# Stick-breaking sums with the later key blocks added up on VectorE first, and the scores copied out of PSUM by ScalarE

## The chip, the cores and the metric

The kernel runs on one core of a Trainium2 chip. Its time is the device time of one execution in microseconds (us), and lower is better. Three runs of the kernel before gave 1179.3, 1180.42 and 1184.48 us, a median of 1180.42. One further execution was recorded by the profiler and took 1179.15 us.

The core has five engines with a queue each, which they work off in order: TensorE (PE in the rows; its weight loads are PEld), VectorE (DVE), ScalarE (ACT), GpSimd (POOL) and SyncE (SP, which issues DMAs). They wait for one another through semaphores. `x.wait_ge(s, n)` holds engine x until semaphore s has reached n, and `.then_inc(s, 1)` raises it when the instruction is done.

## The reference, cut to what matters

The program is one inference step of a hybrid encoder layer: a large input projection, stick-breaking attention (8 heads), a state-space branch, a merge, cross-attention to memory tokens, and a mixture of 16 experts. The change lies in stick-breaking attention alone:

```python
z = jnp.einsum('bqhd,bkhd->bhqk', qb, k_all).astype(f32) * scale
causal = k_pos[None, :] < q_pos[:, None]
log_keep = jnp.where(causal, jax.nn.log_sigmoid(-z), 0.0)
after = lax.cumsum(log_keep, axis=3, reverse=True) - log_keep
w = jnp.where(causal, jnp.exp(jax.nn.log_sigmoid(z) + after), 0.0)
return jnp.einsum('bhqk,bkhd->bqhd', w.astype(v_all.dtype), v_all)
```

For each query, `after` is the sum of log_keep over all later keys up to the query. With l = softplus(z) = -log_keep, the weight is w = exp(z - S), where S at a key is the sum of l over that key and all later ones. There are 512 prompt tokens, and 64 sample tokens that also see 512 cached keys.

## The kernel before, in words

Keys lie on the 128 partitions and queries along the row. A **unit** u is one piece of this work, 1280 values wide. Units 0 to 7 are the eight heads of the prompt: four key blocks kc of 128 keys, for which only the queries from block kc on count, so they are 512, 384, 256 and 128 wide. Units 8 and 9 are the sample tokens, four heads each, with five key blocks of 256 columns. `keycols(u, kc)` gives the place and width of a block. A unit passes through these steps:

- `scores(u)`, TensorE, lines 2875 to 2896: z into PSUM, columns 0 to 1279.
- `z_copy(u)`, VectorE, line 2190: z out of PSUM into `ZSB[u % 6]`.
- `mask(u)`, GpSimd, lines 1664 and 1668: entries that aren't causal get a large negative number.
- `softplus_log(u)`, ScalarE, lines 1819, 1821 and 1823: Abs, Exp and Ln into `LB[u % 2]`.
- `log_sum(u)`, VectorE, line 2194: max(z, 0) is added, which makes l.
- The copy of l, rounded to the format of the fast product (fp32r), into `LBH[u % 2]`, GpSimd, line 1677. `log_low(u)`, VectorE, line 2200, then leaves the rest, l minus its rounded copy, in `LB`. A product with both is nearly as exact as fp32.
- `sums(u)`, TensorE, lines 2911, 2915 and 2916: S into PSUM, columns 1536 to 2815. For key block kc this is a product of a triangle of ones with the block's own l, and a product of a full matrix of ones with each later block j. A block of 256 or more columns takes two fp32r products (high, low); the last one, 128 wide, is a plain fp32 product. That is 12 fp32r and 4 fp32 products in units 0 to 7, and 30 fp32r products in units 8 and 9.
- `u_op(u)`, VectorE, line 2207: z - S. Exp of it by ScalarE, line 1829. `values(u)`, TensorE, line 2928: the product with V for two units.

All engines walk the units in one loop over i, with fixed offsets. TensorE at step i does scores(i), sums(i - 2), then filling work (rows of V by `v_rows`, line 2765, while i < 5), and at even i from 4 on values(i - 4). scores(i) waits until z_copy(i - 1) has emptied its PSUM columns. VectorE does log_low(i - 2), z_copy(i), log_sum(i - 1), u_op(i - 2). ScalarE does the Exp of unit i - 3, softplus_log(i), then the copies of filling work (`kv_out`, line 1786) and at i = 2 and 6 a rounding of a weight tile (line 486, `split_high`). GpSimd does mask(i), then the rounded copy of unit i - 1. At i = 4 the last v_rows has to be copied out by ScalarE before values(0) starts. At i = 10 and later TensorE does `x_rows`, products of the next stage (line 2765 too); x_rows(3) is the first one behind the loop.

## Time and profile before

| what | before |
|---|---|
| runs | 1179.3, 1180.42, 1184.48 us |
| profiled execution, its own time | 1179.15 us |
| its span, first instruction to last | 1177.4 us |
| TensorE busy | 1122.1 us, 95% |
| VectorE busy | 805.8 us, 68% |
| ScalarE busy | 608.2 us, 52% |
| GpSimd busy | 124.5 us, 11% |
| attention loop | from 79.9 us (scores(0)) to 209.15 us (x_rows(3)) |

A row of the timeline has the start in us, the length in us, engine, line, operation, output and inputs, and how many instructions are merged in it. In brackets stands how long the engine had been idle, and who ended that. A TensorE instruction is shown with its latency, so neighbours overlap: what one costs is the distance to the next start. The granted clock 1.00 is 2.4 GHz; lower means are stretches partly at 1.2 GHz.

### The profile page before, as it was taken

Reading aid. Unit: us, or ns where it says so; the run is one execution under the profiler, and the core shown is the slowest. Engines: PE = TensorE matmul, PEld = TensorE weight load, DVE = VectorE, ACT = ScalarE, POOL = GpSimd, SP = SyncE. Lnnn points to the kernel's source line nnn. Section 1 sums busy time; section 2 is a strip of 40 time slices with the busy share of each in tenths; the row PEclk is TensorE's granted clock in tenths of the full one; section 3 lists DMA queues with packets and bytes.
Section 4 is the critical chain, followed back from the end, with each engine's and each line's share of the span. In section 5 each row is a group of like instructions: output and inputs, shape, how many; then the busy total and the mean of one; then the engine's idle time right before and its main releaser. Section 6 shows DMA issues by size and latency. Waiting matters only on the chain.

```text
span 1177.4 us, 18680 instructions
## 1 busy us (share of the span) xinstructions
PE 1122.1 (95%) x7757; PEld 1014.3 (86%) x7766; DVE 805.8 (68%) x993; ACT 608.2 (52%) x807; POOL 124.5 (11%) x148
## 2 busy tenths in 40 slices
PE   6999999999999899899999999999899999999995
PEld 6988789999987799899999999989767878788884
DVE  6324665865968887987535733534589998899895
ACT  6334463335397576643215523312166768677773
POOL 2002431000245000000000000000001000000032
PEclk9999999999999999999999999999799999999998
DMA  9431110323120344442627602201799999999988
GB/s 300 136 120 37 37 41 1 109 72 121 30 55 1 87 123 117 133 151 76 220 72 239 225 3 72 73 1 55 292 353 382 421 419 386 375 400 390 375 274 200
DMA packets 94655, 205.26 MB, mean 174 GB/s; under 512 B 4336, under 2 KB 70040, under 8 KB 81640
## 3 DMA queue, kind: packets, MB, share of 16 engines
q1 hardware_dynamic: 85792, 173.88, 41.6%
q0 software_dynamic: 5584, 19.81, 5.7%
q10 hardware_dynamic: 3192, 10.34, 2.2%
q8 instruction: 63, 1.03, 0.4%
q14 instruction: 24, 0.20, 0.0%
HBM read 182.41 MB, written 21.61 MB: 173 GB/s over the span
## 4 chain that ended last, share of the span: by engine, by line
PE 75%; DVE 9%; ACT 8%; issue 4%; DMA 3%; ACTq 0%; POOL 0%; SPq 0%; DVEq 0%; POOLq 0%
PE ps L2765 34%; PE ps L3101 10%; PE ps L1112 6%; DVE buf_r L1046 4%; ACT buf_r L1039 3%; PE ps L1122 3%; PE ps L3290 2%; PE ps L3306 2%; DMA buf<-in_w_gate_e 1%; PE ps L2886 1%; ACT buf_r L507 1%; DVE buf_r L1261 1%; PE ps L2915 1%; PE ps L2928 1%; PE ps L2916 1%
## 5 line engine op out<-in xcount | busy, mean ns | idle before, releaser
L2765 PE MATMUL ps<-buf_r,buf_r 128*128 128x288 f32 (+1 forms) x3312 | 435.7, 291 | 6.2 <-ACT buf L1812 2.6
L2765 PEld LDWEIGHTS ps<-buf_r,buf_r 128*128 128x128 f32 x3312 | 423.4, 189 | 10.3 <-issue 6.7
L1046 DVE TENSOR_TENSOR buf_r<-buf,buf_r 128x2048 fp32r<-128x2048 f32 x92 | 205.1, 2284 | 0.0
L1112 PE MATMUL ps<-buf_r,buf_r 128*128 128x512 f32 x720 | 174.6, 397 | 0.0
L1039 ACT CAST buf_r<-buf 128x2048 fp32r<-128x2048 f32 x92 | 170.8, 1909 | 0.0
L1112 PEld LDWEIGHTS ps<-buf_r,buf_r 128*128 128x128 f32 x720 | 133.2, 188 | 29.7 <-issue 0.5
L3101 PE MATMUL ps<-buf_r,buf_r 128*128 128x288 f32 x1008 | 140.2, 299 | 9.3 <-ACT buf L1977 4.4
L3101 PEld LDWEIGHTS ps<-buf_r,buf_r 128*128 128x128 f32 x1008 | 137.3, 192 | 11.1 <-issue 9.2
L492 DVE TENSOR_TENSOR buf_r<-buf,buf_r 128x2048 fp32r<-128x2048 f32 (+1 forms) x33 | 74.5, 2262 | 36.2 <-ACT buf_r L486 36.1
L486 ACT CAST buf_r<-buf 128x2048 fp32r<-128x2048 f32 (+1 forms) x37 | 69.7, 1883 | 56.7 <-PE ps L2789 39.7
L1122 PE MATMUL ps<-buf_r,buf_r 128*128 128x512 f32 x384 | 89.8, 389 | 0.5 <-DVE buf_r L1289 0.5
L1122 PEld LDWEIGHTS ps<-buf_r,buf_r 128*128 128x128 f32 x384 | 72.0, 188 | 15.8 <-DVE buf_r L1289 0.9
L507 ACT CAST buf_r<-ps 128x512 fp32r<-128x512 f32 (+2 forms) x41 | 30.0, 731 | 75.8 <-PE ps L1096 63.2
L2365 DVE TENSOR_TENSOR buf_r<-buf,buf_r 128x512 fp32r<-128x512 f32 (+1 forms) x60 | 53.1, 911 | 7.8 <-ACT buf_r L1895 3.3
L638 ACT ACTIVATE buf<-buf 128x1024 f32<-128x1024 f32 (+1 forms) x22 | 23.2, 1056 | 36.7 <-DVE buf L2686 18.7
L1312 POOL DMA_INDIRECT buf<-hn_rows,buf x16 | 17.2, 1073 | 233.9 <-DVE buf L706 133.6
L2190 DVE COPY buf<-ps 128x1280 f32<-128x1280 f32 x10 | 14.9, 1491 | 36.9 <-PE ps L2886 31.8
L507 ACT CAST buf_r<-buf 128x1024 fp32r<-128x1024 f32 (+4 forms) x20 | 19.0, 948 | 40.8 <-DVE buf L2515 34.1
L1702 POOL TENSOR_TENSOR buf<-buf,buf 128x1024 f32<-128x1024 f32 x10 | 28.6, 2863 | 53.0 <-ACT buf L1930 53.0
L1819 ACT ACTIVATE buf<-buf 128x1280 f32<-128x1280 f32 x10 | 12.7, 1274 | 40.1 <-POOL buf L1664 31.0
L1261 DVE TENSOR_TENSOR buf_r<-ps,buf_r 128x1024 fp32r<-128x1024 f32 x15 | 18.4, 1225 | 18.7 <-ACT buf_r L507 18.7
L2104 ACT ACTIVATE buf<-ps 128x288 f32<-128x288 f32 x16 | 6.6, 410 | 46.8 <-PE ps L2765 46.8
(367 smaller groups left out, 1521.6 us busy)
## 6 DMA issues: line engine op xcount, KB each, us to landing
buf<-in_w_gate_e SPq DMA_DIRECT2D x32, 1024.0 KB, 8.2
buf<-in_w_up_e SPq DMA_DIRECT2D x32, 1024.0 KB, 7.5
buf<-in_w_down_e SPq DMA_DIRECT2D x32, 1024.0 KB, 7.6
buf<-in_w_in SPq DMA_DIRECT2D x16, 1024.0 KB, 5.5
buf<-in_w_in SPq DMA_DIRECT2D x17, 512.0 KB
buf<-in_w_mem_kv SPq DMA_DIRECT2D x8, 1024.0 KB, 6.2
y_rows<-buf ACTq DMA_DIRECT2D x14, 512.0 KB, 7.1
buf<-in_x_prompt SPq DMA_DIRECT2D x8, 512.0 KB, 5.3
```

The lines of the kernel that those rows point to most:

```text
L486: nc.scalar.copy(w_hi(n), tile_view(RAW[n % NRAW], n)).then_inc(wh_ready, 1)
L492: nc.vector.tensor_tensor(r32(raw), raw, w_hi(n), ALU.subtract).then_inc(wl_ready, 1)
L507: nc.scalar.copy(r32(hi), src).then_inc(ah_ready, 1)
L1039: nc.scalar.copy(e_hi(t), e_raw(t)).then_inc(wh_ready, 1)
L1046: nc.vector.tensor_tensor(e_lo(t), e_raw(t), e_hi(t), ALU.subtract).then_inc(wl_ready, 1)
L1112: last = nc.tensor.matmul(bank(b), r32(a[:, k, :]), w[:, i, :], start=(k == 0 and j == 0), stop=(k == KD - 1 and j == 2))
L1122: last = nc.tensor.matmul(bank(5 + c), r32(a[:, k, :]), w[:, i, 512 * c:512 * (c + 1)], start=(k == 0 and j == 0), stop=(k == 3 and j == 2))
L1261: nc.vector.tensor_tensor(r32(GT[e % 2]), bank(0, 2).rearrange("p (c n) -> p c n", c=KD), r32(GTH[e % 2]), ALU.subtract).then_inc(al_ready, 1)
L1702: nc.gpsimd.tensor_tensor(CE[v % 2], CE[v % 2], bc(XC[:, 10 + g, c * P:(c + 1) * P].unsqueeze(1), [P, 8, P]), ALU.mult).then_inc(ce_ready, 1)
L2365: return nc.vector.tensor_tensor(r32(out), raw, r32(high), ALU.subtract).then_inc(m_low, 1)
L2765: last = nc.tensor.matmul(out, a, b, start=(k == 0 and j == 0), stop=(k == len(parts) - 1 and j == 2))
L3101: last = nc.tensor.matmul(out, r32(a[:, k, :]), r32(b[:, k, :]), start=(first and k == 0 and j == 0), stop=(k == 3 and j == 2), skip_group ...
```

## The change

After `log_sum`, VectorE adds the key blocks that lie later, column block by column block, into 512 more columns of `LB`. `sums(u)` then takes one product with ones per key block on these added-up columns, in place of one per later block. The rounded copy and `log_low` work on the longer tile. GpSimd now waits for four signals per unit (`RAW_STEPS`). The copy of z out of PSUM moves from VectorE's queue to ScalarE's, ahead of the Exp of unit i - 3. The tiles `LB`, `LBH` and one of `ZSB` lie elsewhere in memory, which brings waits on `mt_stored`, the end of a store of an earlier stage (issued at 53.75 us in the trace).

```diff
-        LB = [A.view(1280) for _ in range(2)]
+        LATER = 512
+        LB, LBH = [A.view(1280 + LATER)], [A.view(1280 + LATER)]
+        A.back(base)
+        LB.insert(0, A.view(1280 + LATER))
+        LBH.insert(0, A.view(1280 + LATER))
         ZSB.append(A.view(1280))
-        A.back(base)
-        LBH = [A.view(1280) for _ in range(2)]
...
+        def sums_later(u, kc):
+            if u < SBH:
+                return {0: [(1408, 3, P)], 1: [(1024, 2, 2 * P)], 2: [(896, 1, P)], 3: []}[kc]
+            return {0: [(256, 2, P), (1536, 2, P)], 1: [(1536, 2, P)], 2: [(1280, 2, P)], 3: [(1024, 2, P)], 4: []}[kc]
...
+                    pool.wait_ge(mt_stored, 16)
+                    pool.wait_ge(sp_raw, RAW_STEPS * u + RAW_STEPS)
+                    nc.gpsimd.tensor_copy(r32(LBH[u % 2]), LB[u % 2]).then_inc(lh_ready, 1)
...
+            def z_copy(u):
+                act.wait_ge(z_psum, u + 1)
+                if u == 3:
+                    act.wait_ge(mt_stored, 16)
+                if u == 4:
+                    act.wait_ge(out_stored, 16 * 2)
+                if u >= 6:
+                    act.wait_ge(pv_psum, 2 * ((u - 6) // 2 + 1))
+                nc.scalar.copy(ZSB[u % 6], ps[:, 0:1280]).then_inc(z_copied, 1)
...
             for i in range(U_ + 3):
+                if i < U_:
+                    z_copy(i)
                 if i >= 3:
...
             def log_sum(u):
                 dve.wait_ge(l_ready, u + 1)
+                lb, done = LB[u % 2], RAW_STEPS * u
+                nc.vector.scalar_tensor_tensor(out=lb[:, 0:1280], in0=ZSB[u % 6], scalar=0.0, in1=lb[:, 0:1280],
                                                op0=ALU.max, op1=ALU.add).then_inc(sp_raw, 1)
+                dve.wait_ge(sp_raw, done + 1)
+                if u < SBH:
+                    nc.vector.tensor_copy(lb[:, 1408:1536], lb[:, 512:640]).then_inc(sp_raw, 1)
+                    nc.vector.tensor_tensor(lb[:, 1280:1408], lb[:, 1152:1280], lb[:, 896:1024], ALU.add).then_inc(sp_raw, 1)
+                    dve.wait_ge(sp_raw, done + 3)
+                    pair_ = lambda at, step: lb[:, at:at + 2 * step].rearrange("p (b n) -> p b n", n=step)[:, :, 0:P]
+                    nc.vector.tensor_tensor(pair_(1536, P), pair_(640, P), pair_(1024, 2 * P), ALU.add).then_inc(sp_raw, 1)
+                else:
+                    nc.vector.tensor_tensor(lb[:, 1280:1536], lb[:, 768:1024], lb[:, 1024:1280], ALU.add).then_inc(sp_raw, 1)
+                    dve.wait_ge(sp_raw, done + 2)
+                    nc.vector.tensor_tensor(lb[:, 1536:1792], lb[:, 512:768], lb[:, 1280:1536], ALU.add).then_inc(sp_raw, 2)
...
-                for k0, k1 in ((0, 896), (1024, 1280)) if u < SBH else ((0, 1280), ):
+                for k0, k1 in ((0, 896), (1024, 1792)) if u < SBH else ((0, 1792), ):
...
             for i in range(U_ + 2):
                 if i >= 2:
                     log_low(i - 2)
-                if i < U_:
-                    z_copy(i)
                 if 1 <= i <= U_:
                     log_sum(i - 1)
...
-                    for j in range(kc, nk):
...
+                    nc.tensor.matmul(own, TSUF_R, high[:, o:o + n], start=True, stop=False)
+                    last = nc.tensor.matmul(own, TSUF_R, low[:, o:o + n], start=False, stop=(kc == nk - 1))
+                    parts = sums_later(u, kc)
```

TensorE, sums(0), all its products. `buf_104_r` is the triangle and `buf_105_r` the ones in fp32r, `buf_58` and `buf_55` are ones and triangle in fp32. Before:

```order
L2915 MATMUL ps<-buf_120_r,buf_104_r 128x512
L2916 MATMUL ps<-buf_117_r,buf_104_r 128x512
L2915 MATMUL ps<-buf_120_r,buf_105_r 128x384
L2916 MATMUL ps<-buf_117_r,buf_105_r 128x384
L2915 MATMUL ps<-buf_120_r,buf_105_r 128x256
L2916 MATMUL ps<-buf_117_r,buf_105_r 128x256
L2911 MATMUL ps<-buf_117,buf_58 128x128
L2915 MATMUL ps<-buf_120_r,buf_104_r 128x384
L2916 MATMUL ps<-buf_117_r,buf_104_r 128x384
L2915 MATMUL ps<-buf_120_r,buf_105_r 128x256
L2916 MATMUL ps<-buf_117_r,buf_105_r 128x256
L2911 MATMUL ps<-buf_117,buf_58 128x128
```

This is key blocks 0 and 1; two fp32r products and two fp32 ones follow for blocks 2 and 3. After, again from the start of sums(0), with all of its products:

```order
L2937 MATMUL ps<-buf_120_r,buf_104_r 128x512
L2938 MATMUL ps<-buf_119_r,buf_104_r 128x512
L2947 MATMUL ps<-buf_120_r,buf_105_r 128x384
L2947 MATMUL ps<-buf_119_r,buf_105_r 128x384
L2937 MATMUL ps<-buf_120_r,buf_104_r 128x384
L2938 MATMUL ps<-buf_119_r,buf_104_r 128x384
L2950 MATMUL ps<-buf_120_r,buf_105_r 128x256
L2950 MATMUL ps<-buf_119_r,buf_105_r 128x256
L2937 MATMUL ps<-buf_120_r,buf_104_r 128x256
L2938 MATMUL ps<-buf_119_r,buf_104_r 128x256
L2943 MATMUL ps<-buf_119,buf_58 128x128
L2935 MATMUL ps<-buf_119,buf_55 128x128
```

The later blocks of block 0 come in one pair 384 wide, and those of block 1 in one pair 256 wide. Twelve products are left of sixteen: two fp32 ones and a pair 256 wide are gone.

ScalarE, steps 5 and 6 of the loop. Before (1829 is the Exp of unit i - 3, 486 the rounding of a weight tile):

```order
L1829 ACTIVATE buf_116<-buf_116 128x1280
L1819 ACTIVATE buf_118<-buf_123 128x1280
L1821 ACTIVATE buf_118<-buf_118 128x1280
L1823 ACTIVATE buf_118<-buf_118 128x1280
L1829 ACTIVATE buf_119<-buf_119 128x1280
L1819 ACTIVATE buf_117<-buf_114 128x1280
L1821 ACTIVATE buf_117<-buf_117 128x1280
L1823 ACTIVATE buf_117<-buf_117 128x1280
L486 CAST buf_73_r<-buf_71 128x2048
```

After (1834 is the copy of z, 1853 the Exp, 488 the rounding):

```order
L1834 COPY buf_123<-ps 128x1280
L1853 ACTIVATE buf_116<-buf_116 128x1280
L1841 ACTIVATE buf_117<-buf_123 128x1280
L1843 ACTIVATE buf_117<-buf_117 128x1280
L1845 ACTIVATE buf_117<-buf_117 128x1280
L1834 COPY buf_114<-ps 128x1280
L1853 ACTIVATE buf_121<-buf_121 128x1280
L1841 ACTIVATE buf_119<-buf_114 128x1280
L1843 ACTIVATE buf_119<-buf_119 128x1280
L1845 ACTIVATE buf_119<-buf_119 128x1280
L488 CAST buf_73_r<-buf_71 128x2048
```

The copy of z for step i now stands behind everything that ScalarE does in step i - 1.

## Rows read from the trace of the kernel before

**Rows 1.** The page, busy time: engine, us, share of the span, instructions.
```profile
PE 1122.1 (95%) x7757; PEld 1014.3 (86%) x7766; DVE 805.8 (68%) x993; ACT 608.2 (52%) x807; POOL 124.5 (11%) x148
```
**Rows 2.** Busy time by stretch: from:to, length, PE, PEld, DVE, ACT, POOL, PEclk, DMA.
```profile
135.00:150.00 15.00, 13.28 (x59) 8.67 (x60) 8.09 (x8) 5.87 (x7) 3.51 (x6) 0.85 0.19 64
```
**Rows 3.** The chain of waits, loop step 4: start, us, what.
```profile
127.46 1.50 DVE buf L2190
```
**Rows 4.** Timeline of TensorE, sums(0) in step 2.
```profile
105.42 0.50 PE L2915 MATMUL ps<-buf_r,buf_r 128*128 128x512 f32 x1
...
106.58 0.39 PE L2911 MATMUL ps<-buf,buf 128*128 128x128 f32 x2
...
106.98 0.34 PE L2916 MATMUL ps<-buf_r,buf_r 128*128 128x384 f32 x1
...
107.15 0.28 PE L2915 MATMUL ps<-buf_r,buf_r 128*128 128x256 f32 x1
...
107.27 0.28 PE L2916 MATMUL ps<-buf_r,buf_r 128*128 128x256 f32 x1
...
108.21 5.90 PE L2765 MATMUL ps<-buf_r,buf_r 128*128 128x256 f32 x48
```
**Rows 5.** Timeline of TensorE, steps 9 to 13.
```profile
177.75 6.62 PE L2765 MATMUL ps<-buf_r,buf_r 128*128 128x288 f32 x48
187.87 2.38 PE L2928 MATMUL ps<-buf,buf 128*64 128x512 f32 x16
190.18 6.62 PE L2765 MATMUL ps<-buf_r,buf_r 128*128 128x288 f32 x48
200.22 6.52 PE L2765 MATMUL ps<-buf_r,buf_r 128*128 128x288 f32 x48
...
209.15 6.09 PE L2765 MATMUL ps<-buf_r,buf_r 128*128 128x288 f32 x44
```
**Rows 6.** Timeline of all engines, step 4.
```profile
125.00 2.42 PE L2886 MATMUL ps<-buf,buf 64*128 64x512 f32 x8
...
129.10 2.16 POOL L1664 TENSOR_SCALAR_AFFINE_SELECT buf<-buf 128x128 f32<-128x128 f32 x4 [5.56 <-DVE buf L2190]
...
130.14 3.07 PE L2765 MATMUL ps<-buf_r,buf_r 128*128 128x256 f32 x24
...
135.48 3.97 PE L2928 MATMUL ps<-buf,buf 128*64 128x512 f32 x16 [2.26 <-ACT buf L1786]
```
**Rows 7.** The same, steps 5 and 6.
```profile
139.38 2.42 PE L2886 MATMUL ps<-buf,buf 64*128 64x512 f32 x8
...
141.84 1.49 DVE L2190 COPY buf<-ps 128x1280 f32<-128x1280 f32 x1 [7.92 <-PE ps L2886]
...
145.57 1.27 POOL L1677 CAST buf_r<-buf 128x1280 fp32r<-128x1280 f32 x1
...
148.35 0.50 PE L2915 MATMUL ps<-buf_r,buf_r 128*128 128x512 f32 x1 [1.24 <-DVE buf_r L2200]
```
**Rows 8.** Timeline of GpSimd and VectorE, masks of steps 0 and 1.
```profile
83.96 1.03 POOL L1664 TENSOR_SCALAR_AFFINE_SELECT buf<-buf 128x128 f32<-128x128 f32 x4 [29.62 <-DVE buf L2190]
...
96.14 4.21 POOL L1664 TENSOR_SCALAR_AFFINE_SELECT buf<-buf 128x128 f32<-128x128 f32 x4 [11.15 <-DVE buf L2190]
...
97.31 2.38 DVE L492 TENSOR_TENSOR buf_r<-buf,buf_r 128x2048 fp32r<-128x2048 f32 x1
```
**Rows 9.** Groups by line and shape, ScalarE, whole span: count, then busy us and mean ns.
```profile
L1930 ACT ACTIVATE buf<-ps 128x1024 f32<-128x1024 f32 x10 | 10.2, 1022 | 7.5 <-PE ps L3045 7.5
```
**Rows 10.** The same groups, 78 to 212 us, all engines.
```profile
L1819 ACT ACTIVATE buf<-buf 128x1280 f32<-128x1280 f32 x10 | 12.7, 1274 | 40.1 <-POOL buf L1664 31.0 <-POOL buf L1668 6.8 <-PE ps L2911 2.3
...
L2200 DVE TENSOR_TENSOR buf_r<-buf,buf_r 128x896 fp32r<-128x896 f32 x8 | 8.7, 1091 | 3.6 <-POOL buf_r L1677 3.6
...
L1790 ACT COPY buf<-ps 128x512 f32<-128x512 f32 x9 | 4.8, 593 | 13.2 <-PE ps L2861 13.2
...
L2200 DVE TENSOR_TENSOR buf_r<-buf,buf_r 128x256 fp32r<-128x256 f32 x8 | 3.3, 418 | 0.0
```

More of the change, by code:

```diff
@@ L1817, in softplus_log @@
                     act.wait_ge(s_psum, u - 1)
-                lb = LB[u % 2]
+                lb = LB[u % 2][:, 0:1280]
                 nc.scalar.activation(lb, ZSB[u % 6], ACT.Abs).then_inc(z_abs, 1)
@@ L2906, in sums @@
                     o, n = keycols(u, kc)
-                    for j in range(kc, nk):
-                        oj, nj = keycols(u, j)
-                        out = ps[:, 1536 + o + n - nj:1536 + o + n]
-                        if nj == P:
-                            last = nc.tensor.matmul(out, TSUF if j == kc else ONES, LB[u % 2][:, oj:oj + nj],
-                                                    start=(j == kc), stop=(j == nk - 1))
-                        else:
-                            m = TSUF_R if j == kc else ONES_R
-                            nc.tensor.matmul(out, m, high[:, oj:oj + nj], start=(j == kc), stop=False)
-                            last = nc.tensor.matmul(out, m, low[:, oj:oj + nj], start=False, stop=(j == nk - 1))
+                    own = ps[:, 1536 + o:1536 + o + n]
+                    if n == P:
+                        last = nc.tensor.matmul(own, TSUF, LB[u % 2][:, o:o + n], start=True, stop=True)
+                        continue
+                    nc.tensor.matmul(own, TSUF_R, high[:, o:o + n], start=True, stop=False)
+                    last = nc.tensor.matmul(own, TSUF_R, low[:, o:o + n], start=False, stop=(kc == nk - 1))
+                    parts = sums_later(u, kc)
+                    for at, blocks, step in parts:
+                        out = own[:, n - P * blocks:n] if u < SBH else own
+                        if u < SBH and kc == 2:
+                            last = nc.tensor.matmul(out, ONES, LB[u % 2][:, at:at + P], start=False, stop=True)
+                            continue
+                        for a in (high, low):
+                            if step == P:
+                                last = nc.tensor.matmul(out, ONES_R, a[:, at:at + P * blocks], start=False,
+                                                        stop=(a is low and at == parts[-1][0]))
+                            else:
+                                last = nc.tensor.matmul(out.rearrange("p (b n) -> p b n", n=P), ONES_R,
+                                                        a[:, at:at + blocks * step].rearrange("p (b n) -> p b n", n=step)[:, :, 0:P],
+                                                        start=False, stop=(a is low))
                 last.then_inc(s_psum, 1)
```

14 lines of the change are left out of this document (3 added, 11 removed).

## The prediction

> **What bounds the kernel now.** I read the page first: TensorE is busy for 95% of the span [rows 1], so the reader is to see that only time on TensorE, or time for which it waits, can move the end. The second view is the busy time by stretch. The attention loop runs from 79.9 us (scores(0)) to 209.15 us (x_rows(3)), and in its stretch from 135 to 150 us TensorE is busy for 13.28 of 15 us at a mean granted clock of 0.85, so for a part of it at the lower level, 1.2 GHz [rows 2]. The third view is the chain of waits: it stays on TensorE for most of the loop and leaves it at 127.46 us, for the copy of z by VectorE and what follows on it [rows 3]. The fourth is the timeline of the places where it leaves. There are two real stalls. At step 4 values(0) starts at 135.48 after 2.26 us of idleness, released by the last copy of filling work on ScalarE [rows 6]. At step 6 sums(4) starts at 148.35 after 1.24 us, released by log_low(4) on VectorE [rows 7]. From step 7 on TensorE has no idle row at all. So the loop is bound by TensorE's own work, broken by two latency chains of which ScalarE and GpSimd are part. Both sides of the change count: less work for TensorE, and another chain.
>
> **Part 1, fewer products (a gain on TensorE).** In sums(0) the distance from the first fp32 row at 106.58 to the row at 106.98 holds one fp32 product and the start of a 384-wide one. The distance from 106.98 to 107.15 is one 384-wide product, 0.17 us, so the fp32 product costs 0.23 us. From 107.15 to 107.27 is one 256-wide product, 0.12 us. The whole unit takes 105.42 to 108.21, 2.79 us [rows 4]. A unit of 0 to 7 loses two fp32 products and a pair 256 wide: 2 x 0.23 + 2 x 0.12 = 0.70 us; I take 0.68, since the starts are rounded. Eight units: 5.4 us. For the sample units, x_rows(1) starts at 190.18 and takes 6.62, and x_rows(2) starts at 200.22, so the 30 products of sums(9) take 3.42 us, 0.115 each [rows 5]. Ten of thirty go: 1.15 us a unit, 2.3 us for two. Removed in all: 7.7 us of TensorE's work. Nothing is added there. One of the kept pairs reads its columns with a gap between blocks, which no row shows: bounds are 0 and, if such a pair took twice its 0.23 us, 8 x 0.23 = 1.8 us; I take 0, because the number of columns is the same as in the row beside it.
>
> **Part 2, VectorE.** It loses ten copies of 1.49 us [rows 7]. It gains per unit the additions (128, 128 and 256 columns, or twice 256) and 512 more columns in log_low. The 896-wide and the 256-wide rows of log_low differ by 0.67 us for 640 columns, 1.05 ns each [rows 10], so log_low grows by 0.53 us to 1.97. Three additions cost at most 3 x 0.42 = 1.26 us, the whole 256-wide row each, and at least 512 x 1.05 ns = 0.54 us; I take 0.95, the middle, as they wait for each other. VectorE's load stays as it was (-1.49 + 0.53 + 0.95 = 0.0 us a unit). But both sit in the latency from Ln to sums(u).
>
> **Part 3, GpSimd.** The rounded copy goes from 1280 to 1792 columns. By the row, 1.27 us [rows 7], it becomes at most 1.27 x 1.4 = 1.78 and at least 1.27; I take 1.75. Its masks took 2.16 us at 129.10 [rows 6] but 1.03 us at 83.96, where VectorE was idle, and 4.21 us at 96.14, with VectorE's 2.38 us subtraction of two operands beside them [rows 8]. At 129.10 log_sum(3) ran beside them, queued right behind the copy of z. Now the copy of z comes from ScalarE, and log_sum(i - 1) is done earlier, right after Ln of unit i - 1, while ScalarE still copies. So I expect masks nearer 1.03 than 2.16 us except at step 6, where log_sum(5) and its additions fall on them; both ends are kept.
> The Trainium skill ("SBUF — State Buffer", section "SBUF: two separate sides") says that VectorE and GpSimd share a pair of ports as an exclusive lock, held for a whole instruction, and that VectorE operations with two SBUF inputs take part in it. The three mask rows agree with it. The rule speaks against this change, since the added copy and additions are such holders, and by it masks stay at 2.16 us or above wherever they meet; that result is rival B, which is priced from the rows.
>
> **Part 4, ScalarE.** It takes over the copy of z. Its 1024-wide reads of PSUM take 1.02 us [rows 9] and its 512-wide ones 0.59 us [rows 10], so 0.84 ns a column and 1.23 us for 1280. Bounds: 1.02 below, and 1.49 above, VectorE's copy of the same [rows 7]. What is queued behind it: the Exp of unit i - 3, then Abs, Exp and Ln of unit i, 3 x 1.27 = 3.8, with gaps 3.9 us [rows 10]. Who waits for it: mask(i), and scores(i + 1), whose PSUM columns it frees. In its turn it now stands behind all of ScalarE's step i - 1. The new waits on mt_stored cost nothing: the store was issued 26 us before the loop begins (the time stands with the change).
>
> **The walk, with 0.1 us for each hand-over.** Steps 2 to 4 hold three sums; two are done before scores(4), which so starts at 123.6 for 125.00 [rows 6] and ends at 126.0. ScalarE: copy of z(4) to 127.3, Exp of unit 1 to 128.6 (the mask beside it), three functions to 132.4, last kv_out to 132.8. TensorE: sums(2) 2.1, v_rows 2.9, ready at 131.0. Values(0) starts at 132.8, 2.7 us earlier, with 1.8 us of stall for 2.26. I keep the slow clock behind it: its row shows 3.97 us for what takes 2.38 at 187.87 [rows 5, 6].
> Step 5: scores(5) ends at 139.2. Copy of z to 140.5, mask to 141.6, rounded copy to 143.4, log_low(4) to 145.4; sums(4) starts at 145.5, 2.85 us earlier. TensorE was ready at 143.6 (sums(3) 2.1, scores(6) 2.35), so this stall grows from 1.24 to 1.9 us: that chain kept its length, the shorter copy and mask pay for the longer rounded copy and log_low, and TensorE's gain of 0.68 us in sums(3) is lost in it.
> Steps 6 to 9: ScalarE is now nearly as slow as TensorE. Per step it has 1.23 + mask 1.1 to 1.5 + 3.9 + hand-overs, 6.7 us, and 1.9 us more at step 6 (line 486). TensorE stalls about 0.3 us before scores(8) (copy of z(7) done at 156.3), 0.3 before sums(6) and 0.6 before values(4), 1.2 us in all where there was none. From sums(4) to x_rows(0) it was 148.35 to 177.75 = 29.4 us [rows 5, 7]; four sums less, 2.7, and 1.2 more make 27.9. x_rows(0) starts at 173.4, 4.3 us earlier. Sums(8) and sums(9) add 2.3, rounded down to 2.2: x_rows(3) at 202.65 for 209.15.
> **The sum: -6.5 us.** In terms of Part 1: -7.7 for the products, -0.5 for the shorter stall of step 4, +0.7 at step 6, +1.2 for the small stalls, -0.2 of rounding. Behind the loop all work follows TensorE's, so I let the gain pass to the end. The profiled execution's own time is 1179.15, so 1172.6 us. That execution lies 1.3 us under the median of the runs shown (1180.42), within their scatter; I add nothing for it.
>
> **Rivals.**
> A, the forecast: -6.5, own range -8 to -5.
> B, masks held at 2.16 us everywhere by VectorE's additions and log_low. For it: rows 6 and 8. Against it: log_sum comes earlier now. It lengthens each of the chains of steps 4 to 9; the same walk with 2.16 puts x_rows(3) at 206.6, so -2.5 and 1176.6 us.
> C, the small stalls lower the clock again. A fall costs 1.6 us, 3.97 - 2.38 [rows 5, 6]. For it: three new stalls within 8 us. Against it: each is far under the 1.24 us of the smallest one that was followed by slow rows. Two more falls, 3.2 us: -3.3, 1175.8 us.
> D, one of the two falls of before does not come back, since it follows how long TensorE idles: -6.5 - 1.6 = -8.1, 1171 us. The stall of step 4 is shorter than before, which speaks for it; that of step 6 is longer.
> The Trainium skill ("TensorE: Matmul & The Clock Gate", "What's actually happening") says that the gate goes by activity in a window that runs free of the program. By it, where a fall lands is partly chance, and so C and D both stay open though the stalls are nearly the same. The two falls in the trace agree with it as far as two can.
> E, the other side: ScalarE becomes the bound of steps 5 to 9. Its place is the copy of z(i + 1), which waits behind Ln of unit i. Before, it took 35.9 us from the copy of z(5) at 141.84 [rows 7] to x_rows(0) at 177.75 [rows 5], 7.2 a step. The loop is 2.5 us ahead when z(5) is copied and gains 2.2 behind step 9, so it turns slower once these five steps take (35.9 + 4.7) / 5 = 8.1 us each; the walk has 34.1 / 5 = 6.8. With every upper end at once (copy 1.49, mask 2.16, rounded copy 2.3, a fall at each of the five stalls) the walk puts x_rows(3) at 211.4: +2.3, 1181.4 us.
>
> **How the numbers follow.** Chances: A 0.53, D 0.12, B 0.17, C 0.11, E 0.07. The forecast is A's, 1172.6. 0.5% is 5.9 us, about what a measurement of this kernel can tell from no change. All of D and 0.38 of A lie beyond it: 0.50 faster. The rest of A (0.15), B and C make 0.43 for the same, and E 0.07 for slower. The range reaches from 1168.5 (D with both falls gone, -9.7, and a little for the scatter) to 1178.5 (B and C together, -1, about half of E left out).
>
> **What the profile after would show.** Part 1: sums(0) at 2.1 us, start to next start, and sums(9) at 2.3. Part 3: rounded copy 1.75 us; masks near 1.0 (A) or 2.2 (B). Part 4: the copy of z 1.2 us. Walk: values(0) at 132.8, sums(4) at 145.5, x_rows(0) at 173.4, x_rows(3) at 202.7; two stretches below clock 1.00 in the loop (A), one (D), three or more (C). It would be wrong if x_rows(0) came no earlier than 177 (ScalarE's chain longer than I walked it), if the gapped pair were slower than its neighbour, or if x_rows(3) came 6.5 us earlier and the end did not.

## The result and the profile after

| | median | lowest to highest | runs |
|---|---|---|---|
| before | 1181.03 us | 1178.11 to 1184.48 | 8 |
| after | 1174.2 us | 1171.2 to 1176.67 | 8 |

The ratio is 0.9941, with a 95% interval of 0.9924 to 0.9959. By this ratio it takes 7.0 us less than before (5 to 9), the medians are 6.8 us apart, and the forecast was 6.5 us less. The profiled execution took 1174.3 us (before 1179.15), its span is 1172.6 us (before 1177.4). The two profiles are thus only 4.85 us apart. The profile of before lies 1.9 us under the median of its kernel, and this will matter below.

First the page's busy times after, against [rows 1]:

```profile
PE 1116.9 (95%) x7698; PEld 1008.7 (86%) x7698; DVE 805.5 (69%) x1011; ACT 620.6 (53%) x817; POOL 116.7 (10%) x148
```

TensorE lost 5.2 us of busy time, VectorE nothing. ScalarE gained 12.4, ten copies. GpSimd lost 7.8 us although its rounded copies grew by 4.3 (from 12.6 to 16.9): its masks lost 12.

The groups by line and shape, 78 to 206 us, of after (columns as in [rows 10]):

```profile
L1689 POOL CAST buf_r<-buf 128x1792 fp32r<-128x1792 f32 x10 | 16.9, 1689 | 7.0 <-DVE buf L2223 7.0
...
L1834 ACT COPY buf<-ps 128x1280 f32<-128x1280 f32 x10 | 12.3, 1226 | 14.4 <-PE ps L2912 10.5 <-PE ps L2920 3.9
...
L1674 POOL TENSOR_SCALAR_AFFINE_SELECT buf<-buf 128x128 f32<-128x128 f32 x32 | 10.3, 360 | 79.9 <-ACT buf L1834 79.9
```

and the masks of before in the same view:

```profile
L1664 POOL TENSOR_SCALAR_AFFINE_SELECT buf<-buf 128x128 f32<-128x128 f32 x32 | 20.2, 666 | 78.4 <-DVE buf L2190 78.4
```

The 32 masks of the prompt take half the time. The timeline of after, all engines (the loop begins with its first row; L2937 begins a sums unit, L2964 is values, L2791 rows of V or x_rows, L2228 log_low, L2211 log_sum, L2235 u_op, L2240 a copy that VectorE has at step 5 as filling work):

```profile
79.28 2.39 PE L2912 MATMUL ps<-buf,buf 64*128 64x512 f32 x8 [0.92 <-ACT buf L1802]
...
104.83 0.50 PE L2937 MATMUL ps<-buf_r,buf_r 128*128 128x512 f32 x1
...
106.94 5.90 PE L2791 MATMUL ps<-buf_r,buf_r 128*128 128x256 f32 x48
...
131.89 1.49 DVE L2211 SCALAR_TENSOR_TENSOR buf<-buf,buf 128x1280 f32<-128x1280 f32 x1 [0.32 <-ACT buf L1845]
132.16 2.37 PE L2964 MATMUL ps<-buf,buf 128*64 128x512 f32 x16 [1.56 <-ACT buf L1798]
...
136.93 1.23 ACT L1834 COPY buf<-ps 128x1280 f32<-128x1280 f32 x1 [4.81 <-PE ps L2912]
138.30 1.04 POOL L1674 TENSOR_SCALAR_AFFINE_SELECT buf<-buf 128x128 f32<-128x128 f32 x4 [8.73 <-ACT buf L1834]
...
139.20 1.49 DVE L2235 TENSOR_TENSOR buf<-buf,ps 128x1280 f32<-128x1280 f32 x1 [4.90 <-PE ps L2935]
...
139.27 1.70 POOL L1689 CAST buf_r<-buf 128x1792 fp32r<-128x1792 f32 x1
...
140.61 0.68 DVE L2240 COPY buf<-ps 128x512 f32<-128x512 f32 x1
...
141.21 1.95 DVE L2228 TENSOR_TENSOR buf_r<-buf,buf_r 128x896 fp32r<-128x896 f32 x2
...
143.21 0.50 PE L2937 MATMUL ps<-buf_r,buf_r 128*128 128x512 f32 x1 [1.70 <-DVE buf_r L2228]
...
174.53 6.59 PE L2791 MATMUL ps<-buf_r,buf_r 128*128 128x288 f32 x48
...
203.53 6.62 PE L2791 MATMUL ps<-buf_r,buf_r 128*128 128x288 f32 x48
```

The reader is to see five things. Sums(0) takes 104.83 to 106.94, 2.11 us for 2.79 [rows 4]. Log_sum(4) runs at 131.89, five microseconds before the copy of z(5), so the mask at 138.30 has no such VectorE operation beside it and takes 1.04 us for 2.16 [rows 6]. The stalls are 1.56 us at step 4 (2.26 before [rows 6]) and 1.70 at step 6 (1.24 before [rows 7]). And x_rows(3), the first work behind the loop, starts at 203.53 for 209.15 [rows 5]; 0.60 of these 5.62 us come from ahead of the loop, where nothing was changed. Last, what holds sums(4) at step 6: the rounded copy is done at 140.97, but VectorE comes to log_low(4) only at 141.21, straight from u_op(3), which had waited for sums(3), and a copy behind it. So there the chain over mask and rounded copy, which the prediction walked, ended 0.2 us before VectorE's own queue.

Now the clock. Stretches of after (columns as in [rows 2]; in rows of TensorE alone PE, PEclk, DMA share and GB/s are left), then of before:

```profile
135.00:150.00 15.00, 13.30 (x62) 9.50 (x61) 9.31 (x11) 11.30 (x10) 7.06 (x12) 0.89 0.09 33
150.00:165.00 15.00, 15.00 (x82) 12.91 (x82) 10.26 (x14) 12.33 (x10) 4.85 (x7) 0.77 0.16 52
165.00:180.00 15.00, 15.00 (x109) 14.06 (x106) 9.80 (x10) 10.17 (x9) 2.04 (x2) 0.89 0.00 1
...
144.00:145.00 1.00, 1.00 (x5) 0.50 0.00 0
...
159.00:161.00 2.00, 2.00 (x7) 0.50 0.00 0
...
171.00:173.00 2.00, 2.00 (x6) 0.50 0.00 0
```

```profile
150.00:165.00 15.00, 15.00 (x99) 12.49 (x98) 10.28 (x10) 10.98 (x9) 7.81 (x12) 0.92 0.23 80
165.00:180.00 15.00, 15.00 (x115) 13.32 (x115) 10.63 (x9) 8.15 (x8) 5.46 (x4) 1.00 0.00 1
```

A clock of 0.50 is 1.2 GHz. From such rows I add up the time at the lower level: a stretch of mean clock c has a share 2 x (1 - c) of it. Before it is 6.8 us in the loop, behind the two stalls. After it is 13.6: 3.4 from 143.7, 6.8 from 157.2, 3.4 from 171. In the last two TensorE has no idle row. At 1.2 GHz its work takes nearly twice as long: sums(6) of after, all of it at the lower level, took 4.14 us (159.67 to 163.81) for the 2.32 of sums(5) at full clock (151.67 to 153.99), so 0.44 of such time is lost. I count half, the upper end: 6.8 us lost for 3.4 before. The loop times without the low clock are so too short by up to 0.4 us for before, 0.8 for after and 1.0 for a kernel with 17 us. With the clock taken out (length less half of the low stretch) the loop goes from 129.27 - 3.4 = 125.9 to 124.25 - 6.8 = 117.4 us, 8.4 less; the clock gives 3.4 of it back, and 5.0 are left in this pair of profiles. (With 0.44 in place of a half it is 8.0 less and 3.0 back.)

### The profile page after: what moved, and what is told of

The parts are those of the page before. It is cut to its first block, busy times and chain, and to the rows that moved or that the text cites. A ratio compares the mean times of both kernels' runs of the same rounds, so it can differ in the third digit from the quotient of the medians.

```text
span 1172.6 us, 18594 instructions
## 1 busy us (share of the span) xinstructions
PE 1116.9 (95%) x7698; PEld 1008.7 (86%) x7698; DVE 805.5 (69%) x1011; ACT 620.6 (53%) x817; POOL 116.7 (10%) x148
## 3 DMA queue, kind: packets, MB, share of 16 engines
q8 instruction: 63, 1.03, 0.4%
## 4 chain that ended last, share of the span: by engine, by line
PE 74%; DVE 10%; ACT 9%; issue 4%; DMA 3%; ACTq 0%; SPq 0%; POOL 0%; DVEq 0%; POOLq 0%
PE ps L2791 34%; PE ps L3137 10%; PE ps L1122 6%; DVE buf_r L1056 4%; ACT buf_r L1049 4%; PE ps L1132 3%; PE ps L3326 2%; PE ps L3342 2%; PE ps L2912 1%; ACT buf_r L509 1%; DVE buf_r L1271 1%; PE ps L3105 1%; PE ps L1106 1%; PE ps L2920 1%; PE ps L3108 1%
## 5 line engine op out<-in xcount | busy, mean ns | idle before, releaser
L2791 PE MATMUL ps<-buf_r,buf_r 128*128 128x288 f32 (+1 forms) x3312 | 435.7, 291 | 6.2 <-ACT buf L1824 2.6
L2791 PEld LDWEIGHTS ps<-buf_r,buf_r 128*128 128x128 f32 x3312 | 423.4, 189 | 10.3 <-issue 6.7
L2235 DVE TENSOR_TENSOR buf<-buf,ps 128x1280 f32<-128x1280 f32 x10 | 14.9, 1489 | 28.4 <-PE ps L2935 20.4
L2287 DVE SCALAR_TENSOR_TENSOR buf<-buf,buf,buf 128x579 f32<-128x579 f32 x36 | 29.6, 822 | 1.3
```

The lines of the kernel that those rows point to most:

```text
L2287: o = nc.vector.scalar_tensor_tensor(out=cv[:, 0:579], in0=xr[:, j:j + 579], scalar=CW[:, j, i:i + 1], in1=cv[:, 0:579], op0=ALU.mult, op1 ...
L2791: last = nc.tensor.matmul(out, a, b, start=(k == 0 and j == 0), stop=(k == len(parts) - 1 and j == 2))
```

## The experiments

Each kernel had 6 or 12 runs, with 17 to 29 of before beside them; the ratio is to those, whose medians were 1181.1 to 1181.52 us (for after it is to the 8 above). The table has what the profiles show of the loop, from the start of scores(0) to that of x_rows(3). "Stalls" are TensorE's idle times before values(0) and sums(4).

| kernel | loop | low clock | loop without it | stalls | median | ratio to before, 95% |
|---|---|---|---|---|---|---|
| before | 129.27 | 6.8 | 125.9 | 2.26, 1.24 | 1181.03 | |
| after | 124.25 | 13.6 | 117.4 | 1.56, 1.70 | 1174.2 | 0.9941 [0.9924, 0.9959] |
| e0_changed_again | 124.76 | 13.6 | 118.0 | 1.56, 1.70 | 1174.64 | 0.9942 [0.9927, 0.9957] |
| e1_copy_only | 131.41 | 13.6 | 124.6 | 1.46, 1.17 | 1180.1 | 0.9988 [0.9976, 1.0] |
| e2_sums_only | 128.76 | 17.0 | 120.3 | 3.20, 3.23 | 1181.46 | 0.9996 [0.9982, 1.001] |
| e3_old_products | 130.47 | 10.2 | 125.4 | 1.47, 1.70 | 1181.52 | 1.0005 [0.999, 1.0019] |
| e4_fill_stalls | 123.09 | 10.2 | 118.0 | 0.17, none | 1173.27 | 0.9932 [0.9911, 0.9952] |
| e5_late_log_sum | 129.13 | 17.0 | 120.6 | 3.06, 3.10 | 1181.47 | 0.9997 [0.9986, 1.0009] |
| e6_kv_early | 121.38 | 10.2 | 116.3 | none | 1174.03 | 0.9936 [0.9921, 0.9951] |
| e7_fill_scores | 130.63 | 17.0 | 122.1 | 0.17, none | 1181.28 | 1.0001 [0.9988, 1.0014] |
| e8_split_sums | 124.69 | 13.6 | 117.9 | 1.57, 0.83 | 1174.33 | 0.9942 [0.9925, 0.9958] |
| e9_split_kv_early | 121.70 | 10.2 | 116.6 | none, 0.83 | 1172.93 | 0.993 [0.9914, 0.9946] |
| e10_before_filled | 130.80 | 10.2 | 125.7 | 0.40, none | 1180.18 | 0.9989 [0.9972, 1.0006] |

The rest of the program adds scatter of its own: scores(0) starts between 79.06 and 82.52, though nothing ahead of it differs. So verdicts go by the medians, and the loop's columns explain them as far as one profile can. Every run also lists the mean granted clock of its whole execution. The medians are 0.980 for e2, 0.9795 for e5, 0.982 for e7, 0.9825 for after, 0.985 for e0, 0.983 to 0.9855 for the others and 0.984 to 0.986 for before.

### e1_copy_only

Before, with the copy of z on ScalarE, ahead of the Exp of unit i - 3. The added lines are ScalarE's, the removed ones VectorE's.

```diff
+            def z_copy(u):
...
+                nc.scalar.copy(ZSB[u % 6], ps[:, 0:1280]).then_inc(z_copied, 1)
...
-                if i < U_:
-                    z_copy(i)
```

> The kernel before with one thing moved: ScalarE copies z out of PSUM, at the place in its queue that the change gives it. Sums, additions and rounded copies are as before. Theory 'work' (the gain is TensorE's fewer products, so this half alone brings little): x_rows(3) 1 to 2 us earlier than before, ratio to before 0.998 to 1.000. Theory 'chain' (the gain is the shorter way from scores to values: a shorter copy, masks at 1.0 instead of 2.2 us): 5 us or more, ratio 0.996 or less. Masks at 1.0 us under both.

Measured 0.9988, 0.1%. The masks fall as they do in after:

```profile
141.11 1.05 POOL L1664 TENSOR_SCALAR_AFFINE_SELECT buf<-buf 128x128 f32<-128x128 f32 x4 [9.49 <-ACT buf L1820]
```

The stalls shrink by 0.9 us together, and without the low clock the loop is 1.3 us shorter. So this half alone shortens a wait and little else: it is what theory 'work' expected of it. The stall of step 6 shrinks by only 0.07 us (1.24 to 1.17) although mask and copy of z are 1.4 us shorter, so that path didn't hold it there.

### e2_sums_only

After, with the copy of z back on VectorE between log_low(i - 2) and log_sum(i - 1). The removed lines are ScalarE's, the added ones VectorE's.

```diff
-                if i < U_:
-                    z_copy(i)
...
                     log_low(i - 2)
+                if i < U_:
+                    z_copy(i)
                 if 1 <= i <= U_:
                     log_sum(i - 1)
```

> The changed kernel with the copy of z back on VectorE, between log_low(i - 2) and log_sum(i - 1). The additions and the shorter sums stay. Theory 'work': most of the gain stays, 4 to 6 us, ratio 0.995 to 0.997, with longer stalls at steps 4 and 6 since masks go back to 2.2 us. Theory 'chain': under 2 us, ratio 0.998 or more.

Measured 0.9996: the fewer products alone give nothing. Theory 'work' wanted 0.995 to 0.997 and is missed here, though e1 and e3 fit it: neither of the two theories holds alone. Its timeline, all engines:

```profile
121.14 3.32 POOL L1689 CAST buf_r<-buf 128x1792 fp32r<-128x1792 f32 x1 [0.37 <-issue]
...
130.83 1.48 DVE L2243 TENSOR_TENSOR buf<-buf,ps 128x1280 f32<-128x1280 f32 x1
131.04 1.68 POOL L1689 CAST buf_r<-buf 128x1792 fp32r<-128x1792 f32 x1
...
135.28 3.44 PE L2974 MATMUL ps<-buf,buf 128*64 128x512 f32 x16 [3.20 <-ACT buf L1798]
...
141.68 1.49 DVE L2214 COPY buf<-ps 128x1280 f32<-128x1280 f32 x1 [6.97 <-PE ps L2922]
143.09 1.48 DVE L2219 SCALAR_TENSOR_TENSOR buf<-buf,buf 128x1280 f32<-128x1280 f32 x1
143.32 2.42 POOL L1674 TENSOR_SCALAR_AFFINE_SELECT buf<-buf 128x128 f32<-128x128 f32 x4 [10.60 <-DVE buf L2214]
```

VectorE copies z, then starts log_sum at 143.09, and the mask, which waited for the same copy, starts at 143.32 and takes 2.42 us. Both stalls grow to 3.2 us, 3.2 more together than in after. The low clock grows to 17.0 us, 10.2 more than in the profile of before.

### e3_old_products

After, with the old products (one per later block), so that only TensorE's saving is missing.

```diff
-                    parts = sums_later(u, kc)
...
+                    for j in range(kc, nk):
+                        oj, nj = keycols(u, j)
+                        out = ps[:, 1536 + o + n - nj:1536 + o + n]
```

> The changed kernel with additions, longer rounded copy, longer log_low and ScalarE's copy, but TensorE's sums take one product per later block as before (the added-up columns are made and not used). Theory 'work': the gain falls to about 1 us, ratio 0.999 (0.998 to 1.001); the difference to the changed kernel is the price of 7.7 us of products. Theory 'chain': ratio stays at 0.994 to 0.996.

Measured 1.0005: taking the products back costs the whole gain. Without the low clock its loop is 8.0 us longer than that of after and 7.4 longer than that of e0 (the forecast's term: 7.7).

### e0_changed_again

The changed kernel once more, for a second profile of it.

> The changed kernel as it is, a second profile and more runs on the chip of this call. Ratio to before 0.992 to 0.996. Falls of the clock behind scores(8) and scores(9) again, if these cause them; elsewhere, if they come by chance.

Ratio 0.9942, the same. Its low clock in the loop is 13.6 us again, but placed otherwise: 157 to 167 and 174 to 178, and none behind the same two stalls of 1.56 and 1.70 us. So within one kernel the place of the falls varies, and stalls of this length don't decide them. What recurs is where the late ones begin: scores(8) starts at 154.69 and scores(9) at 168.63 here, 153.99 and 166.27 in after, and in all twelve profiles that have late falls one begins 2.3 to 5.1 us behind the start of scores(8) and one 3.4 to 5.5 us behind that of scores(9). Only the profile of before has none at either.

### e5_late_log_sum

After, with one more wait on VectorE: log_sum(i - 1) starts only when the copy of z(i) is done. No work is added.

```diff
                 if 1 <= i <= U_:
+                    if i < U_:
+                        dve.wait_ge(z_copied, i + 1)
                     log_sum(i - 1)
```

> The changed kernel with one wait added: VectorE starts log_sum(i - 1) and its additions only when the copy of z(i) is done, so that they fall on the masks of unit i, as they do when VectorE makes that copy itself. No operation is added or removed. Theory 'masks' (the copy's move pays because log_sum gets ahead of the masks; on VectorE it holds them): masks go from 1.0 to 2.4 us, the stalls at steps 4 and 6 from 1.6 and 1.7 to about 3 us each, and most of the gain is lost, ratio to before 0.997 to 1.000. Rival 'only the copy's own 0.3 us and VectorE's load count': ratio stays at 0.994 to 0.996.

Measured 0.9997. All of the gain is gone. Its timeline, all engines:

```profile
129.31 1.28 ACT L1841 ACTIVATE buf<-buf 128x1280 f32<-128x1280 f32 x1 [1.55 <-POOL buf L1674]
...
133.50 3.88 PE L2966 MATMUL ps<-buf,buf 128*64 128x512 f32 x16 [3.06 <-ACT buf L1798]
...
139.90 1.23 ACT L1834 COPY buf<-ps 128x1280 f32<-128x1280 f32 x1 [6.45 <-PE ps L2914]
...
141.16 1.49 DVE L2211 SCALAR_TENSOR_TENSOR buf<-buf,buf 128x1280 f32<-128x1280 f32 x1 [8.22 <-ACT buf L1834]
141.27 2.55 POOL L1674 TENSOR_SCALAR_AFFINE_SELECT buf<-buf 128x128 f32<-128x128 f32 x4 [10.33 <-ACT buf L1834]
...
143.59 1.48 DVE L2235 TENSOR_TENSOR buf<-buf,ps 128x1280 f32<-128x1280 f32 x1
...
143.80 1.68 POOL L1689 CAST buf_r<-buf 128x1792 fp32r<-128x1792 f32 x1
...
145.58 1.95 DVE L2228 TENSOR_TENSOR buf_r<-buf,buf_r 128x896 fp32r<-128x896 f32 x2
...
147.59 0.59 PE L2939 MATMUL ps<-buf_r,buf_r 128*128 128x512 f32 x1 [3.10 <-DVE buf_r L2228]
```

The copy of z is ScalarE's, as in after, and yet the numbers are those of e2: mask 2.55 us, stalls 3.06 and 3.10, low clock 17.0. So what the move of the copy buys is not the copy itself. It lets log_sum run ahead of the masks instead of behind the copy.

What the late log_sum costs differs between the two stalls. At step 4 it is the mask: Abs of unit 4 waits 1.55 us for it, the last kv_out stands behind Abs, Exp and Ln, and the stall grows by 1.50. At step 6 it needn't be. From 141.16 to the end of log_low(4) at 147.53 VectorE works without a gap: log_sum(4), its additions, u_op(3), the copy and log_low(4), 6.4 us. In after, log_sum and additions, 2.4 us of this, ran in VectorE's idle time between 131.89 and 139.20. The held mask and the rounded copy behind it end at 145.48, a tenth of a microsecond before VectorE is free. By these rows either way alone would have made the stall about as long, and no run lengthens one without the other.

### e4_fill_stalls

After, with six products of no use (full matrix of ones, 512 columns, into a free bank) before the wait of step 4 and six before sums(4).

```diff
+                if u == 4:
+                    filler(6)
                 pe.wait_ge(ll_ready, u + 1)
...
+                    pe.wait_ge(kv_rows, 19)
+                    filler(6)
                     pe.wait_ge(kv_rows, 20)
```

> The changed kernel with six products of 512 columns (1.3 us) put into each of TensorE's two stalls, ahead of sums(4) at step 6 and ahead of the wait for the last kv_out at step 4; their results go to a free bank and are not used. Theory 'clock by idleness' (the 14.1 us at the lower clock between 143 and 175 us follow from these stalls): most of that is gone, at 0.5 us saved per us of low clock up to 7 us, at least 3 us faster than the changed kernel, ratio to before 0.990 or less. Rival 'the falls have another cause' (two of the three came in scores(8) and scores(9), where TensorE had no idle row): low stretches stay at scores(8) and scores(9), ratio 0.993 to 0.995.

Measured 0.9932 against 0.9942 for e0; the intervals overlap, and the 3 us of theory 'clock by idleness' (0.990 or less) did not come. The clock from 135 to 150 us is 1.00, and the falls from 157 us on remain. Its stretches:

```profile
135.00:150.00 15.00, 14.85 (x77) 9.88 (x73) 9.44 (x12) 11.54 (x10) 7.06 (x12) 1.00 0.09 32
150.00:165.00 15.00, 14.77 (x95) 12.34 (x93) 12.07 (x16) 13.56 (x12) 4.87 (x7) 0.89 0.22 76
165.00:180.00 15.00, 15.00 (x95) 14.69 (x95) 8.93 (x10) 8.61 (x7) 2.04 (x2) 0.77 0.00 1
```

### e10_before_filled

The same on the kernel before, eight products at step 4 and four at step 6.

```diff
+                if u == 4:
+                    filler(4)
...
+                    pe.wait_ge(kv_rows, 19)
+                    filler(8)
```

> The kernel before with unused 512-column products in its two stalls, eight (1.7 us) ahead of the wait for the last kv_out at step 4 and four (0.9 us) ahead of sums(4) at step 6. Theory 'clock by idleness': both falls of the profile before (135 and 149 us) go, 7 us of low clock, 3 us faster, ratio 0.997. Rival 'the falls only move to the steps behind', as with the changed kernel's fillers: ratio 0.999 to 1.000, falls behind 157 us.

Measured 0.9989, inside what can't be told from no change (the rival's range ends there, and its falls behind 157 us came). The two falls of before are gone from their places, and 10.2 us of low clock stand between 161 and 179 instead:

```profile
135.00:150.00 15.00, 14.88 (x82) 10.36 (x80) 10.17 (x9) 6.14 (x6) 5.92 (x10) 1.00 0.14 51
150.00:165.00 15.00, 15.00 (x96) 12.93 (x93) 11.17 (x11) 11.38 (x9) 7.49 (x10) 0.89 0.23 80
165.00:180.00 15.00, 15.00 (x95) 13.32 (x93) 6.98 (x6) 6.18 (x5) 3.37 (x3) 0.77 0.00 1
```

One fall begins 4.6 us behind the start of scores(8), one 3.4 us behind that of scores(9). So the late falls are not made by the change. They come with the old products too (e1, e3, e10), and it is the one profile of before that has none there.

### e7_fill_scores

e4, with four products over all rows, 512 columns each, between those of scores(8) and of scores(9), whose own use half of the array's rows and 64 columns. The theory was that these thin products let the clock fall.

```diff
+                        if kc == 0:
+                            pe.wait_ge(ysb_ready, u - SBH + 1)
+                        if kc < 4:
+                            for _ in range(1):
+                                nc.tensor.matmul(bank(6 + u - SBH)[:, 0:512], ONES_R, r32(HTH[:, 0, 0:512]), start=True, stop=True)
```

> As the kernel with both stalls filled, and four products of 512 columns and all 128 rows (unused) spread through scores(8) and through scores(9), 0.9 us each, 1.8 us in all. The products of scores(8) and (9) use 64 rows and 64 columns. Theory 'thin products' (the lower clock behind scores(8) and scores(9) comes from these 4.6 us of thin products, not from idleness): the two or three falls after 150 us go, 5.1 us back for 1.8 us spent, ratio 0.990 to 0.992. Rival 'chance of time': falls stay, 1.8 us slower than the kernel with filled stalls, ratio 0.995.

The expectation failed: the falls stayed, the low clock grew from 10.2 to 17.0 us, and the median by 8 us, for eight fillers (eight such take 2.03 us in a row of e10). In the loop it is 7.5 us, and the rows say of what. Between the thin products a filler takes 0.42 us, and a group of eight thin ones 1.03 instead of 0.92 (4.60 for the forty of scores(8) in before), so each filler costs some 0.5 us, 4.1 to 4.5 in all, and the low clock makes the other 3.0 to 3.4:

```profile
155.42 0.49 PE L2926 MATMUL ps<-buf_r,buf_r 128*128 128x512 f32 x1
155.84 1.10 PE L2920 MATMUL ps<-buf,buf 64*128 64x64 f32 x8
156.88 0.50 PE L2926 MATMUL ps<-buf_r,buf_r 128*128 128x512 f32 x1
```

```profile
150.00:165.00 15.00, 14.78 (x71) 12.01 (x70) 9.90 (x14) 11.14 (x10) 3.59 (x8) 0.80 0.23 80
165.00:180.00 15.00, 15.00 (x75) 11.59 (x75) 5.70 (x6) 6.08 (x6) 1.92 (x2) 0.73 0.00 0
180.00:195.00 15.00, 15.00 (x105) 13.62 (x104) 9.83 (x8) 7.69 (x9) 3.37 (x3) 0.90 0.00 1
```

That doesn't clear the thin products. The fillers lengthened the stretches of scores(8) and scores(9) and left the thin products in them, and the falls still begin 4.7 and 3.8 us behind their starts.

### e6_kv_early

e4 without the fillers of step 4. The last v_rows stands ahead of sums(2) and its copy ahead of Abs of unit 4, so nothing is left to wait for; eight fillers before sums(4).

```diff
+                if i == 4:
+                    kv_out(19, V_BANK[9])
                 if i < U_:
                     softplus_log(i)
...
+                if i == 4:
+                    v_rows(9)
                 if 2 <= i < U_ + 2:
                     sums(i - 2)
```

> The changed kernel with the last v_rows of step 4 ahead of sums(2), its copy by ScalarE ahead of softplus_log(4), and eight products of 512 columns (1.7 us, unused) in the stall ahead of sums(4). The stall of step 4 (1.56 us) should go and values(0) start at about 130.6 in the profile's time; ScalarE starts softplus_log(4) some 0.9 us later, so sums(4) gains only about 0.7 us. Expected 0.5 to 1.5 us faster than the changed kernel, ratio 0.992 to 0.994. Rival: the stall only moves to step 6 and nothing is gained.

Both stalls are gone and the profiled loop is 2.9 us shorter than that of after, but the median is 1174.03, 0.9936 against 0.9942 for e0, which can't be told apart. The profile started scores(0) 3.2 us later than that of after, so the profile alone can't say more.

### e8_split_sums

After, with the rounded copy and log_low signalled in two parts (columns 0 to 895, then the rest), and sums(u) starting its own-block products on the first part.

```diff
-                    nc.gpsimd.tensor_copy(r32(LBH[u % 2]), LB[u % 2]).then_inc(lh_ready, 1)
+                    pool.wait_ge(sp_raw, RAW_STEPS * u + 1)
+                    nc.gpsimd.tensor_copy(r32(LBH[u % 2])[:, 0:896], LB[u % 2][:, 0:896]).then_inc(lh_ready, 1)
...
-                pe.wait_ge(ll_ready, u + 1)
+                pe.wait_ge(ll_ready, 2 * u + 1)
...
+                for kc in early:
+                    own_sums(kc)
+                pe.wait_ge(ll_ready, 2 * u + 2)
```

> The changed kernel with the rounded copy and log_low signalled in two parts (columns 0 to 895, then the rest), and sums(u) starting its own-block products of the first part before the second is there. It shortens the way from mask(5) to sums(4) by about 0.8 us on GpSimd and 0.9 us on VectorE. If that way is what holds TensorE (theory 'latency'), the 1.7 us stall of step 6 nearly goes and the kernel is 1 to 2 us faster than the changed one, ratio 0.992 to 0.993. Rival: what is gained at step 6 is lost again at scores(8), which waits for ScalarE's copy of z(7); no difference, 0.994.

Measured 0.9942, the same as after. Its timeline of TensorE:

```profile
143.60 0.50 PE L2939 MATMUL ps<-buf_r,buf_r 128*128 128x512 f32 x1 [0.83 <-DVE buf_r L2232]
...
146.84 2.38 PE L2978 MATMUL ps<-buf,buf 128*64 128x512 f32 x16 [0.84 <-ACT buf L1856]
```

The stall before sums(4) falls from 1.70 to 0.83, and a new one of 0.84 stands before values(2): it needs the Exp of unit 3, which is in ScalarE's queue behind Ln of unit 5 and the copy of z(6). The gain is handed on to the next wait whole. The rival, no difference, is what came, though by values(2) and not by scores(8), which waits 0.22 us.

### e9_split_kv_early

e8 with the early v_rows and kv_out of e6, and no fillers.

> As the kernel with the split sums, and the last v_rows of step 4 ahead of sums(2) with its copy ahead of softplus_log(4), which takes away the stall of step 4 (1.56 us). No filling products. Theory 'latency': 2 to 3 us faster than the changed kernel, ratio 0.991 to 0.993. Rival: ScalarE's queue holds steps 5 to 8 anyway, ratio 0.994.

Measured 1172.93 us, 0.993 [0.9914, 0.9946]. It has the lowest median of all and no useless work (in its profile the stall before values(2) is 1.04), but its interval overlaps that of the changed kernel (0.9942 [0.9927, 0.9957] in e0), so it isn't shown to be faster.

## Why the prediction was right

**The size.** 6.5 us were forecast, 7.0 measured (5 to 9), and 1174.2 us lies in the range; the forecast of 1172.6 was made against a profile 1.9 us under its own median. The terms:

- Part 1, products, -7.7: sums(0) takes 2.11 us for the forecast 2.1, and e3 shows -8.0 (-7.4 against e0) for all ten units and the whole gain with them. For the sample units the forecast took the 6.62 us of x_rows(1), a length with its latency, for a distance. Sums(9) is 3.59 us (196.63 to 200.22), not 3.42, and 2.38 after, so the term is 7.9. The pair with gaps costs nothing extra: it lies within sums(0).
- Part 2, additions and log_low: the forecast said that what matters is the latency from Ln to sums. For sums(4) it isn't: log_sum(4) and its additions were over five microseconds before, and only u_op(3), the copy and log_low(4) stood in the way. The additions end at 134.3, 0.9 us behind log_sum (0.95 forecast), log_low takes 1.95 (1.97).
- Part 3: rounded copy 1.69 us (1.75), masks 1.04 (1.03), and 1.43 at step 6, where additions fell on it, as expected. The mask of 4.21 us in [rows 8] had not only the subtraction beside it but also log_sum, 1.48 us from 95.92. Rival B, masks at 2.16, is refuted for the changed kernel; the masks of the sample units fell too, which I had not priced. But e2 and e5 show that B was near. With log_sum on the masks they take 2.4 to 2.55 us, and the medians of e2 and e5 lose not the 4 us that B was priced at but the whole 7. The loop of e5 is 4.9 us longer than that of after: 3.3 are idle time, and the rest comes with 3.4 us more of low clock, which B's price left out. The 2 us more of the medians lie outside what this pair of profiles shows; the mean clock of e5's runs, 0.9795 for 0.9825 to 0.985 of the changed kernel, points to the clock. And that the masks are what lengthens the stall of step 6 is not shown (see e5).
- Part 4: copy of z 1.23 us (1.23).
- Stall of step 4: 1.56 us for the forecast 1.8. Values(0) starts 52.88 us behind scores(0); the walk had 52.9.
- Stall of step 6: 1.70 for 1.9, so the size was right and the reason only nearly. The walk had the chain over copy of z, mask and rounded copy keep its length and end last; VectorE's own queue ended 0.2 us behind it. Sums(4) starts 63.9 us behind scores(0) for 65.6 in the walk. Of these 1.7 us, 1.6 are the fall at step 4, which the walk had kept and which neither profile of the changed kernel has (rival D).
- Small stalls of steps 7 to 9, +1.2: the profile of after has none of them, e0 one of 0.21 before scores(8).

Measured in the loop of the two profiles, the sum is -7.9 for the products, -0.7 and +0.5 for the two stalls, nothing for small ones, and 3.0 to 3.4 for the clock: -4.7 to -5.1, where the rows have -5.0. The forecast had -6.5.

That 6.5 and 7.0 lie so near each other is in part luck. The forecast charged 1.2 us for small stalls that didn't come and nothing for more low clock, which cost 3 us in this pair; and the medians are 2 us further apart than the profiles, for a reason that no run shows.

**What was wrong in it.** The walk kept the two falls of the clock where they were. The one at step 4 was missing, and 10.2 us of low clock stand between 157 and 174.5, where before had none (rival C, though it was to come from small stalls, and there were none). Sums(4) to x_rows(0) took 31.3 us for 27.9. In this pair of profiles the clock so gave back 3.4 us of 8.4. In its loop the profile of before is unusually clean: 6.8 us low, against 10.2 and 13.6 in e1, e3 and e10, which have the same products (e10 twelve fillers more). Over its whole span it isn't: its mean granted clock is 0.984, where other runs of before have medians of 0.984 to 0.986. That of after, 0.979, is the lowest of its eight runs. So why the profile of before lies 1.9 us under its median stays open.

**Rival E** did not come. ScalarE's chain held: between step 6 and the end of the loop no row of TensorE in after names ScalarE, and one of 0.21 us in e0 does, before scores(8), as do such of 0.22 or 0.23 in e4 and e6 to e9. It is near, though. In e8 the very next thing that TensorE waited for was ScalarE's queue.

**The two halves don't add up.** The copy alone gives 0.1%, the sums alone 0.0%, both 0.6%. Fewer products make TensorE reach its waits earlier, and the added operations on VectorE and GpSimd make the release later. With log_sum on the masks the two stalls grow by 2.9 us together over before (6.4 for 3.5), and the low clock, 10.2 us more than in the profile of before, eats the rest. The runs bear this out: the mean clock of twelve is 0.980 in the middle, for 0.984 of before. With log_sum ahead of them they stay at 3.3 us, and the saving goes through. That needs no other move than the order: e5 differs from after in one wait.

**Left open.** Why the clock falls behind 155 us. It does in twelve of thirteen profiles, in rows where TensorE isn't idle, each time shortly behind the start of scores(8) and of scores(9), and neither filling the stalls ahead (e4, e10) nor fillers between the thin products (e7) takes it away. Whether the thin products bring it on is not shown: no run takes them out, and the one profile of before has them without a fall. Nor is it shown why a filler costs 0.5 us among them. And at step 6 the held mask and VectorE's later log_sum are not told apart.

## What to carry to other kernels

When work is taken from the engine that bounds the kernel, look at the chain that releases it: here 7.7 us of saved products were worth nothing until the chain kept pace. Look for pairs of instructions of VectorE and GpSimd that are released by the same event, and for work that an engine does behind an event though its inputs were there before. Moving it ahead took nothing away here and was worth as much as the saved products: it freed the mask at step 4, and at step 6 it also used time in which VectorE was idle. Before a change is judged from two profiles, write down the time at the lower clock in each, since it can hide or make up half of the effect.
